# One pass over w_v for the sample tile and the first prompt tile

## The reference

```
xn = rms_norm(x, mix_pre_g)                   # x * rsqrt(mean(x*x) + eps) * g
z  = xn @ w_in                                # 1024 x 7168, split into u, v, b, c, x_in, r_a, r_b
v  = layer_norm(gelu(v), sgu_ln_g, sgu_ln_b)  # v = xn @ w_v, 1024 columns of w_in
```

## Time and profile before

| | |
|---|---|
| runs, median | 1675.05 us (1674.32 to 1675.25) |
| profiled execution | 1673.22 us, its span 1671.5 us |
| PE (TensorE) busy | 1615.1 us, 97% of the span |
| DVE (VectorE) busy | 1005.3 us, 60% |
| ACT (ScalarE) busy | 550.0 us, 33% |
| POOL (GpSimd) busy | 695.0 us, 42% |
| mean granted TensorE clock | 0.99 |

### The profile page before, as it was taken

How to read it: one execution, slowest core, us unless ns; L and a number is a source line. 1 busy time by engine, 2 the same in 40 slices (tenths; PEclk the granted TensorE clock), 3 DMA queues, 4 the chain that set the end, 5 groups by cost and what they waited for, 6 DMA issues and landing times. The chain is left out here.

```text
span 1671.5 us, 30860 instructions
## 1 busy us (share of the span) xinstructions
PE 1615.1 (97%) x12892; PEld 1583.1 (95%) x12892; DVE 1005.3 (60%) x1400; ACT 550.0 (33%) x857; POOL 695.0 (42%) x498
## 2 busy tenths in 40 slices
PE   8999999999999999999999899999999999999993
PEld 5889999999999999999999899999999999999993
DVE  7657757577573335134448984444445448677966
ACT  5322332222223333111335443323232234433543
POOL 1011544444544443233533265444444445563663
PEclk9999999999999999999999999999999999999996
DMA  7302010321323336332513122222222324515204
GB/s 237 123 26 76 26 52 33 95 77 33 95 65 120 110 113 217 108 97 75 144 47 127 58 95 77 79 86 89 79 77 77 96 89 140 177 59 165 83 2 152
DMA packets 140605, 157.77 MB, mean 94 GB/s; under 512 B 5996, under 2 KB 127732, under 8 KB 139444
## 3 DMA queue, kind: packets, MB, share of 16 engines
q1 hardware_dynamic: 131844, 151.54, 28.1%
q10 hardware_dynamic: 8624, 4.27, 0.9%
HBM read 118.73 MB, written 37.09 MB: 93 GB/s over the span
## 5 line engine op out<-in xcount | busy, mean ns | idle before, releaser
L367 PE MATMUL ps<-tp,ring_hi 128*128 128x258 f32 x7676 | 1253.3, 284 | 13.1 <-DVE tp L2023 6.3
L367 PEld LDWEIGHTS ps<-tp,ring_hi 128*128 128x128 f32 x7676 | 1069.8, 190 | 15.0 <-issue 12.9
L367 PE MATMUL ps<-tp,ring_lo 128*128 128x258 f32 x3838 | 796.0, 283 | 0.0
L367 PEld LDWEIGHTS ps<-tp,ring_lo 128*128 128x128 f32 x3838 | 606.6, 191 | 0.0
L938 POOL TENSOR_TENSOR ring_lo<-stage,ring_hi 128x512 fp32r<-128x512 f32 (+1 forms) x212 | 320.2, 1518 | 598.3 <-ACT ring_hi L1117 598.0
L938 POOL TENSOR_TENSOR ring_lo<-ring_f,ring_hi 128x512 fp32r<-128x512 f32 (+1 forms) x204 | 294.7, 1456 | 236.2 <-DVE ring_f L1611 108.7
L1117 ACT ACTIVATE ring_hi<-ring_f 128x512 fp32r<-128x512 f32 (+1 forms) x204 | 127.5, 626 | 483.2 <-DVE ring_f L1611 169.0
L1117 ACT ACTIVATE ring_hi<-stage 128x512 fp32r<-128x512 f32 (+1 forms) x212 | 128.7, 618 | 205.6 <-PE ps L367 144.9
L1608 DVE TENSOR_TENSOR ring_f<-stage 128x512 f32<-128x512 f32 (+1 forms) x51 | 40.5, 795 | 189.2 <-PE ps L367 111.4
L367 PE MATMUL ps<-wv_hi_t,tp 128*128 128x512 f32 x256 | 71.7, 397 | 0.0
L1629 DVE TENSOR_TENSOR s_a<-ps,s_a 128x516 f32<-128x516 f32 (+1 forms) x52 | 35.6, 685 | 48.3 <-PE ps L367 47.2
(11 more groups left out here) (227 smaller groups left out, 1320.5 us busy)
## 6 DMA issues: line engine op xcount, KB each, us to landing
stage<-in_w_in SPq DMA_DIRECT2D x24, 1024.0 KB, 5.9
stage<-in_w_gate SPq DMA_DIRECT2D x11, 1024.0 KB, 6.0
stage<-in_w_up SPq DMA_DIRECT2D x11, 1024.0 KB, 5.4
hid_dram<-hq SPq DMA_DIRECT2D x40, 258.0 KB, 3.0
tp_f<-hid_dram SPq DMA_DIRECT2D x20, 516.0 KB, 5.1
stage<-in_w_down SPq DMA_DIRECT2D x8, 1024.0 KB, 5.5
ob_dram<-q SPq DMA_DIRECT2D x16, 258.0 KB, 2.9
ra_dram<-q SPq DMA_DIRECT2D x16, 258.0 KB, 2.1
```

The lines of the kernel that those rows point to most:

```text
L367: ins = pe.matmul(o, w, xc, start=first and n == 0, stop=last and n == 2)
```

## The change

- `v_tile` takes a list of row blocks. The sample tile and the first prompt tile are no longer computed one behind the other: TensorE takes block 0 of the sample, raw transposes of step 1, block 1, norm transposes of step 1, blocks 2 and 3, blocks 0 and 1 of step 1, and then in turn a block of the sample (4 to 7) and a block of step 1 (2 to 4). The transposes of step 2 follow, then blocks 5 to 7 of step 1. From step 2 on the list is as before.
- SyncE loads the scale row once, for 128 rows, as its second load, then block 0, x of step 1, blocks 1 to 7, x of step 2. Its wait for the scaling of step 0 is gone.
- ScalarE squares step 1 ahead of `keep(0)`, into `x_save`, without the wait for the norm transposes; `keep(1)` stands ahead of the split of block 4, and `square(2)` behind that of block 7. `keep(2)` makes the high part ahead of the copy.
- VectorE makes the sample's low part behind block 0, scales step 1 ahead of blocks 1 and 2 (with a new wait for the sample's norm transposes), makes step 1's low part ahead of block 3, and scales step 2 and makes its low part ahead of the loop. In the loop nothing is scaled for i = 0.

```diff
--- before.py
+++ after.py
@@ -387,15 +387,13 @@
                                        x_norm[0:rows, 128 * k:128 * k + 128], ident[0:rows, 0:rows])
                 ins.then_inc(norm_turned, 1)
 
-            def v_tile(i):
+            def v_tile(i, ks=range(KT)):
                 t = V_TILES[i]
                 pe.wait_ge(xn_lo_done, i + 1)
                 if i >= 2:
                     pe.wait_ge(v_gelu, i - 1)
-                for k in range(KT):
+                for k in ks:
                     if i == 0:
-                        if k == 3:
-                            turn_norm(1)
                         pe.wait_ge(wv_lo, k + 1)
                     if t == 8:
                         x_h, x_l = smp_hi[:, k, :], smp_lo[:, k, :]
@@ -405,7 +403,8 @@
                     outs = [ps[0:rows_of(t), 2 * (i % 2) + n, :] for n in range(2)]
                     w_h, w_l = ([w[:, k, 512 * n:512 * n + 512] for n in range(2)] for w in (wv_hi_t, wv_lo_t))
                     ins = three(outs, x_h, x_l, w_h, w_l, k == 0, k == KT - 1)
-                ins.then_inc(v_full, 1)
+                if ks[-1] == KT - 1:
+                    ins.then_inc(v_full, 1)
 
             def turn_consts():
                 pe.wait_ge(raw_copied, 9)
@@ -435,9 +434,22 @@
             pe.wait_ge(consts, 4)
             turn_raw(0)
             turn_norm(0)
+            v_tile(0, [0])
             turn_raw(1)
-            for i in range(9):
-                v_tile(i)
+            v_tile(0, [1])
+            turn_norm(1)
+            v_tile(0, [2, 3])
+            v_tile(1, [0, 1])
+            for k in range(4, KT):
+                v_tile(0, [k])
+                if k < KT - 1:
+                    v_tile(1, [k - 2])
+            turn_raw(2)
+            turn_norm(2)
+            v_tile(1, range(KT - 3, KT))
+            for i in range(1, 9):
+                if i > 1:
+                    v_tile(i)
                 if i + 2 < 9:
                     turn_raw(i + 2)
                     turn_norm(i + 2)
@@ -709,18 +721,12 @@
                 sp.dma_start(stage[STAGE[b]][:, 0:2 * kps(b), :], src).then_inc(stage_in[STAGE[b]], 16)
 
             x_load(0)
-            sp.dma_start(pre_gain[0:NS, :], mix_pre_g[0:1, :].to_broadcast((NS, D))).then_inc(pre_in, 16)
+            sp.dma_start(pre_gain[:, :], mix_pre_g[0:1, :].to_broadcast((128, D))).then_inc(pre_in, 16)
             wv_load(0)
-            wv_load(1)
             x_load(1)
-            wv_load(2)
-            sp.wait_ge(x_scaled, 1)
-            sp.dma_start(pre_gain[:, :], mix_pre_g[0:1, :].to_broadcast((128, D))).then_inc(pre_in, 16)
-            wv_load(3)
-            wv_load(4)
+            for k in range(1, KT):
+                wv_load(k)
             x_load(2)
-            for k in range(5, KT):
-                wv_load(k)
             sp.dma_start(ln_g[0:NS, :], sgu_ln_g[0:1, :].to_broadcast((NS, D))).then_inc(ln_g_in, 16)
             sp.dma_start(ln_b[:, :], sgu_ln_b[0:1, :].to_broadcast((128, D))).then_inc(ln_b_in, 16)
             x_load(3)
@@ -1059,9 +1065,10 @@
             def square(i):
                 rows = rows_of(V_TILES[i])
                 act.wait_ge(x_in[i % 2], 16 * (i // 2 + 1))
-                if i:
+                if i > 1:
                     act.wait_ge(norm_turned, i)
-                act.activation(x_norm[0:rows, :], x_rows[i % 2][0:rows, :], ACT.Square,
+                squares = x_save if i == 1 else x_norm
+                act.activation(squares[0:rows, :], x_rows[i % 2][0:rows, :], ACT.Square,
                                accum_out=small[0:rows, i:i + 1]).then_inc(sumsq, 1)
 
             def wv_split(k):
@@ -1076,9 +1083,8 @@
                     act.activation(xn_prompt(V_TILES[i], 0), turned(6), ACT.Copy).then_inc(xn_hi_done, 1)
 
             def keep(i):
-                if i == 1:
+                if 0 < i < 3:
                     norm_split(i)
-                    square(2)
                 act.wait_ge(raw_turned, i + 1)
                 if i == 0:
                     raw = bank_pair(4, NS).rearrange("p k (g b i) -> p b g k i", g=2, b=2)
@@ -1092,7 +1098,7 @@
                     act.wait_ge(xt_saved, 16 * (i - 1))
                 saved = x_save[:, :].rearrange("p (k n) -> p k n", k=KT)
                 act.activation(saved, bank_pair(4), ACT.Copy).then_inc(raw_copied, 1)
-                if i != 1:
+                if i > 2:
                     norm_split(i)
                 b, gg, off = home(V_TILES[i])
                 act.wait_ge(raw_copied, i + 1)
@@ -1129,13 +1135,14 @@
 
             square(0)
             wv_split(0)
-            wv_split(1)
+            square(1)
             keep(0)
-            wv_split(2)
-            square(1)
-            for k in range(3, KT):
+            for k in range(1, 4):
                 wv_split(k)
             keep(1)
+            for k in range(4, KT):
+                wv_split(k)
+            square(2)
             for i in range(9):
                 if 0 < i < 7:
                     square(i + 2)
@@ -1514,7 +1521,9 @@
                 dve.wait_ge(sumsq, i + 1)
                 link(dve.tensor_scalar(a, small[0:rows, i:i + 1], 1.0 / D, EPS, MUL, ADD))
                 rsqrt(y, a, w)
-                dve.wait_ge(pre_in, 32 if i else 16)
+                dve.wait_ge(pre_in, 16)
+                if i == 1:
+                    dve.wait_ge(norm_turned, 1)
                 dve.scalar_tensor_tensor(x_norm[0:rows, :], x_rows[i % 2][0:rows, :], y, pre_gain[0:rows, :], MUL, MUL).then_inc(x_scaled, 1)
 
             def wv_rest(k):
@@ -1542,16 +1551,18 @@
                 dve.tensor_scalar(v, v, small[0:rows, 36:37], y, SUB, MUL).then_inc(v_norm, 1)
 
             scale_rows(0)
-            for k in range(2):
-                wv_rest(k)
+            wv_rest(0)
             xn_rest(0)
+            scale_rows(1)
+            wv_rest(1)
             wv_rest(2)
-            scale_rows(1)
+            xn_rest(1)
             for k in range(3, KT):
                 wv_rest(k)
-            xn_rest(1)
+            scale_rows(2)
+            xn_rest(2)
             for i in range(9):
-                if i + 2 < 9:
+                if 0 < i < 7:
                     scale_rows(i + 2)
                 if i < 8:
                     v_layer_norm(i)
```

## The result

The changed kernel takes 1686.26 us, the median of four runs (1685.42 to 1688.0), against 1674.95 (1674.32 to 1675.25, four runs): a ratio of 1.0071 (95% interval 1.0058 to 1.0083): slower by some 11 us. The forecast was 1686.2 us, in a range of 1682.5 to 1690.5. The profiled execution took 1687.06 us, its span is 1685.3 and its mean granted clock 0.986 (before 1673.22, 1671.5 and 0.990). TensorE is busy for 1618.5 us, 96% of the span.

A forecast was written before the change was run, and what follows sets the result against it. TensorE was taken to bound the kernel, with v-stage shifts reaching the end. Late norm transposes 8.8, scale row 0.3 and slow clock 2.1 sum to 11.2 us on 1675.05: 1686.2 us, range 1682.5 to 1690.5.

The forecast's parts named there:

- TensorE stands for block 3: Start of v stage: block 3's low part is ready at 20.2, so TensorE stands from 18.1 to 20.25.
- step 1's matmuls end later by: V stage: step 1 ends 1.4 us later than 38.69; the scale row adds 0.3.
- What bounds it: From 80 to 100 us TensorE is fully busy, so a v-stage shift of its work goes through to the end.
- The start: VectorE's order puts step 1's low part (17.85 to 19.0) before block 3's (20.2); old 1.60 hole gone, new holes replace it.
- a second loss at the start: Rival, 0.23: clock rises later than 14.3 or falls in the hole at 18.1; 1687.9 to 1689.4 us, middle 1688.5.
- the late rise: Part of a rival: clock rises 3 us later at the start, slowing block 1 and the norm transposes, +1.7 us.
- The chain: Step 3's scaling waits behind step 2's low part and the sample's layer norm until 48.3; TensorE stands 7.35 us.
- The clock: After the long hole the clock stays low for 4.4 us, costing 2.1 us; bounds 0 to 3.0.
- The weighing of transposes: At the start: by the trace row transposes help the clock rise; by the skill's rule they hold it back, giving 1688.5.
- The scale row: Wide broadcast row first in the load queue: start 0.95 us later at worst, -0.3 at best; +0.3 taken.
- chain covered: Rival, 0.05: fourth scaling ready within TensorE's 5.1 us of work, no hole before step 3's norm transposes; 1673.4 or 1676.8 us.
- nothing changes: Rival, 0.01: w_v's arrival bounds the pass, so the time stays level.

The follow-up runs named there:

- second profile: The changed kernel run again with no edit: median 1688.13 us, ratio 1.0077; its profiled execution took 1685.28 us.
- block 3 first: Changed kernel with the low part of w_v's block 3 ahead of step 1's low part on VectorE: 1683.43 us, ratio 1.0052.
- three runs with a filled hole: Changed kernel with needless work before step 3's norm transposes: 30 matmuls in two runs, 1688.29 and 1687.36 us; 72 transposes, 1687.95 us.
- the last experiment: Chain-cut kernel with late sample layer norm, scale row split: 8 rows as second load, 128 behind x of step 1: 1676.33 us.
- loop-alone profile: Kernel before, with VectorE scaling step 2 and making its low part ahead of the loop, scaling nothing for step 0: 1677.21 us.
- last two kernels: Chain-cut kernel with the sample's layer norm moved to step 4 of VectorE's loop, 1677.84 us; the same with the narrow scale row first, 1676.33 us.
- chain-cut kernel: Changed kernel, block 3's low part ahead of step 1's, step 3 squared early, fourth scaling ahead of step 2's low part: 1675.63 us.
- fourth-scaling kernel: Changed kernel with step 3's scaling ahead of the sample's layer norm and its square behind step 2's high part: 1681.77 us.
- loads-alone kernel: Kernel before, with only the changed order of loads: 1675.3 us, ratio 1.0006.

## Why the prediction was right

| step of the prediction | forecast | measured, changed kernel (second profile) |
|---|---|---|
| block 0 of the sample starts | 10.1 | 10.02 |
| TensorE stands for block 3 | 18.1 to 20.25 | until 20.60, 2.12 (2.12) |
| step 1's matmuls end later by | 1.4 + 0.3 | 3.34 (1.71) |
| hole ahead of step 3's norm transposes | 7.35 | 8.40 (8.41) |
| slow clock after it | 2.1 | 2.09 (2.11) |
| scale row | +0.3 of 0.95 | about 0.1 |
| profiled execution, difference | 11.2 | 13.84 (12.06) |

*What bounds it.* Right: a shift in the v stage goes through to the end one to one. With block 3 first, step 1 ends 3.96 us earlier (38.07 against 42.03) and the profiled execution is 3.89 shorter (1683.17 against 1687.06). The three runs with a filled hole are the exception: what they gained in the v stage was lost at the hole near 1409 us, to a collision of VectorE with GpSimd and a fall of the clock. All behind the v stage shifts as one only where neither comes in between.

*The start.* Right as a mechanism: low part of step 1 at 18.19 and block 3's at 19.33, by the forecast order. The size was right in the second profile. In the first the clock fell at the 2.12 us hole and cost some 1.5 us more. That is half of the rival "a second loss at the start": the fall in the hole, which it priced at 1.5, without the late rise (the first full-speed matmuls stand at 14.65, before at 14.33). With that price the time is 1687.7, and five executions of nine lie around it, at 1687.06 to 1688.64. I had argued against it from one hole of 1.60 that left the clock alone; one execution of a hole says little.

*The chain.* Right, and the largest term: the waits end at VectorE's scaling, the sample's layer norm starts at 40.23 (38.60 in the second), taking away the order takes away the hole. It was sized 1.0 us short. Of that 0.87 is the one small operation of 1.02 us (0.89 in the second profile), in the term taken as 6.74: the prediction had copied the layer norm's length from a stretch in which GpSimd stood beside none of its small operations, and did not ask what GpSimd would be doing when it came later. The rest is the time until ScalarE's copy starts. (35.9 + 1.0 + 1.14 is 38.04; the prediction wrote 38.15, which brought it 0.1 nearer.)

*The clock.* Right to a tenth: the three fills took this term out of the v stage (1.7 to 2.3 us). The weighing of transposes came out for the row: 72 of them kept the clock up, against what the Trainium skill, "TensorE: Matmul & The Clock Gate", "Part 4: PE-mode transpose", would give.

*The scale row.* Beyond its slot in the queue, its price was nearer none: block 0 behind it landed at 6.98, against 6.9 by the pace of plain loads. The slot itself is worth 1.06 us to the sample's first matmul, as the last experiment shows.

The rivals "chain covered" and "nothing changes" fell. That the median comes within 0.1 us is partly luck: it lies in the gap between the two clusters, some 10.5 and 13.1 us above the kernel before, where no execution lies. The chain's shortfall of 1.0 does not show in it, because the two profiled executions differ by more (12.06 and 13.84) than the medians do (11.31): the profiled execution before lay 1.83 below its median.

## What to carry to other kernels

When two passes are merged, look at what the first one released when it ended: here the sample's gelu came 11.9 us later, and the work that used to lie beside 11.2 us of matmuls stood in front of the next scaling with three blocks to cover it. On an engine with an order written by hand, small work that becomes late costs in full what lies behind it; placing it later only helps where the idle time of the steps that follow (3.9 us here) exceeds it. And where an engine waits for two results that a second engine makes one behind the other (as at the hole of 1.60), changing their order only changes which of them the profile names. Last, ask of every stretch of work that moves in time what the engines beside it will then be doing: here one VectorE operation grew by 0.6 to 0.9 us in seven profiles, and another by 0.6 to 0.7 in three, each time beside a GpSimd operation that it had not met before.

## What the runs showed of the hardware

- A hole of 2.12 us ahead of block 3 stands in six profiles; the granted clock fell behind it in five and not in the sixth, and the changed kernel has one of each. One of 1.69 lowered it in the loop-alone profile; 1.60 did not in the kernel before, and 1.45 and 1.29 did not. Of the holes of 3.04 and 3.02 in the last two kernels, the first left the transposes behind it at full speed (1.09 us) and the second did not (1.97). A fall costs 1.4 to 1.6 us behind the holes of 1.7 to 2.4 us, 2.1 behind the long one and 2.7 behind the one of 3.02. Single executions of one kernel scatter by 2 to 6 us, as much as most edits here are worth; how much of that is the clock, the profiles don't show.
- Transposes alone kept the full clock: 72 in 8.0 us at 1.00.
- A VectorE operation can wait beside one of GpSimd's. In seven profiles (the changed kernel twice, block 3 first, the three with a filled hole, the chain-cut kernel) one small operation between 38.5 and 43 us took 0.74 to 1.08 us instead of 0.15. Each starts while GpSimd's select on `ws_rows` (1.09 to 1.11 us) runs and ends within 0.01 us of it. The scaling of 2.11 in the fourth-scaling kernel, the addition of ln_b in the loads-alone kernel (2.00 instead of 1.21) and the products of 1.28 to 1.44 near 1387 us start beside a GpSimd operation too. Not every VectorE operation waits: the statistics of 0.66 us in the loop-alone kernel and a `TENSOR_SCALAR` of 0.14 in the chain-cut kernel run beside the same select at their usual length.
